# A two-block decoder kernel: the end of each RWKV head pair placed beside the beginning of the next, with one table for the weight products behind the steps

## The reference, cut to what matters

```python
w = -softplus(-(w0 + tanh(wd) @ w2)) - 0.5;  decay = exp(-exp(w))
a = sigmoid(a0 + ad @ a2)
kk = heads(k * k_k);  kk = kk * rsqrt(max(sum(kk * kk), 1e-24))
k = k * (1.0 + (a - 1.0) * k_a)
o = rwkv7_scan(r, decay, k, v, -kk, kk * a)     # state = state*w + sa*b + v*k, o = state @ r
mean = mean(o); var = mean(square(o - mean))    # per head of 64
o = (o - mean) * rsqrt(var + GN_EPS) * ln_w + ln_b
yb = (o + sum(r * k * r_k) * v) * silu(bz)
```

## Time and profile before

| | us |
|---|---|
| median of 3 runs | 3160.08 (3158.09 to 3163.82) |
| profiled execution | 3159.61 |
| its span, first to last instruction | 3157.7 |
| TensorE busy | 3028.3 (96%), mean granted clock 0.984 |
| DVE busy | 1664.5 (53%) |
| ACT busy | 1357.8 (43%) |

### The profile page before, as it was taken

The page is one execution under the profiler, slowest core; times in us unless marked ns, Lnnn a source line. Parts: engine busy times, 40 slices in busy tenths (PEclk is TensorE's granted clock), DMA queues, the critical chain, the costliest instruction groups (busy, mean ns, idle before and its releaser), DMA issues.

```text
span 3157.7 us, 44484 instructions
## 1 busy us (share of the span) xinstructions
PE 3028.3 (96%) x19042; PEld 2586.2 (82%) x19042; DVE 1664.5 (53%) x1975; ACT 1357.8 (43%) x1563; POOL 76.0 (2%) x186
## 2 busy tenths in 40 slices
PE   7999999889999999999999999999999999999998
PEld 6888877868998878879889879888888888888886
DVE  5555555547655555645455456655555444444444
ACT  5333333434454445444444444444444444444333
POOL 4000000000100000000000000000000000000000
PEclk9999999999999999999999999999999999999999
DMA  6333333336666555556655645666656666666554
GB/s 188 108 108 109 108 110 110 106 102 185 175 191 195 163 153 153 187 173 173 179 169 173 188 137 146 175 189 187 193 187 180 183 183 183 187 184 198 188 187 146
DMA packets 355098, 516.32 MB, mean 164 GB/s; under 512 B 18224, under 2 KB 137156, under 8 KB 354132
## 3 DMA queue, kind: packets, MB, share of 16 engines
q1 hardware_dynamic: 354132, 510.27, 53.8%
q0 software_dynamic: 768, 3.20, 0.4%
HBM read 511.29 MB, written 2.11 MB: 163 GB/s over the span
## 4 chain that ended last, share of the span: by engine, by line
PE 92%; ACT 4%; DVE 3%; issue 1%; DMA 0%; SPq 0%; DVEq 0%; ACTq 0%
PE gp L1361 20%; PE gp L1363 20%; PE gp L1362 20%; PE gp L1370 8%; PE gp L1371 8%; PE gp L1372 8%; PE ps L1522 4%; PE ps L1412 1%; PE ps L1483 1%; PE ps L1508 1%; ACT w_hi L548 1%; PE ps L1469 1%; DVE arena L877 1%; DVE w_lo L883 0%; ACT L540 0%
## 5 line engine op out<-in xcount | busy, mean ns | idle before, releaser
L883 DVE TENSOR_TENSOR w_lo<-w_raw,w_hi 128x1024 fp32r<-128x1024 f32 (+2 forms) x976 | 1168.2, 1202 | 944.5 <-ACT w_hi L548 943.1
L548 ACT ACTIVATE w_hi<-w_raw 128x1024 fp32r<-128x1024 f32 (+2 forms) x976 | 1012.6, 1040 | 1229.6 <-PE gp L1363 916.7
L1361 PE MATMUL gp<-w_hi,h_hi 128*128 128x512 f32 x1920 | 768.7, 400 | 0.0
L1362 PE MATMUL gp<-w_hi,h_lo 128*128 128x512 f32 x1920 | 758.3, 395 | 0.0
L1363 PE MATMUL gp<-w_lo,h_hi 128*128 128x512 f32 x1920 | 757.9, 395 | 0.0
L1370 PE MATMUL gp<-h_hi,w_hi 128*128 128x256 f32 x2080 | 613.9, 295 | 8.6 <-DVE w_lo L883 6.8
L1371 PE MATMUL gp<-h_lo,w_hi 128*128 128x256 f32 x2080 | 586.8, 282 | 0.0
L1372 PE MATMUL gp<-h_hi,w_lo 128*128 128x256 f32 x2080 | 586.2, 282 | 0.0
L1363 PEld LDWEIGHTS gp<-w_lo,h_hi 128*128 128x128 f32 x1920 | 360.2, 188 | 87.9
L1361 PEld LDWEIGHTS gp<-w_hi,h_hi 128*128 128x128 f32 x1920 | 360.3, 188 | 87.0
L1362 PEld LDWEIGHTS gp<-w_hi,h_lo 128*128 128x128 f32 x1920 | 360.4, 188 | 84.3
(11 more groups left out here) (282 smaller groups left out, 2024.7 us busy)
## 6 DMA issues: line engine op xcount, KB each, us to landing
w_raw<-in_w_in SPq DMA_DIRECT2D x384, 512.0 KB, 3.7
w_raw<-in_w_ffn_gate SPq DMA_DIRECT2D x88, 512.0 KB, 4.4
w_raw<-in_w_ffn_up SPq DMA_DIRECT2D x88, 512.0 KB, 4.3
w_raw<-in_w_ffn_down SPq DMA_DIRECT2D x88, 512.0 KB, 3.7
w_raw<-in_w_in SPq DMA_DIRECT2D x136, 256.0 KB, 3.2
w_raw<-in_w_in SPq DMA_DIRECT2D x128, 192.0 KB, 2.8
w_raw<-in_w_mem_kv SPq DMA_DIRECT2D x32, 512.0 KB, 4.0
w_raw<-in_w_o SPq DMA_DIRECT2D x32, 512.0 KB, 4.0
```

Source lines behind the costliest of these rows:

```text
L548: act.activation(w_hi[:, slot, 0:size], w_raw[:, slot, 0:size], ACT.Copy).then_inc(sem("hi_done"), 1)
L883: dve.tensor_tensor(w_lo[:, slot, 0:size], w_raw[:, slot, 0:size], w_hi[:, slot, 0:size].bitcast(F32), ALU.subtract)\
L1361: pe.matmul(o, xh, wh, start=(k == 0), stop=False)
L1362: pe.matmul(o, xl, wh, start=False, stop=False)
```

## The change

1. Each pair's part is cut in three functions on each engine: `pair_begin(p)` (lora, sigmoids, kk, root, decays, and on DVE the products up to `kr_ready`), `pair(p)` (products, levels, chunks), and the end. The end of pair p - 1 is spread: the mean, the deviation, its square, the variance and the second root stand inside `pair_begin(p)`; DVE's `pair_end(p - 1)` stands behind `k_read` of pair p, ACT's `y_hi` behind the g copy of level 1, DVE's `low_y` ahead of level 2. The bonus product goes ahead of the last output product, and DVE reads it at once.
2. The units of all pairs are one list of 128 units (512 quarters). `plan_fill` says how many quarters are dealt out by each step; TensorE takes them by quarters, ACT and DVE by the whole units that this number holds. Nothing drains between pairs.
3. `on_heads` makes each term for both heads before the next term.
4. The evacuation of a B block waits for `kr_ready` in place of `shift_read`, and buffers are placed anew in the arena.

The core of the diff:

```diff
+STEPS = ([("prod", 2)] + [(f"{s}{l}", q) for l in range(1, LEVELS) for s, q in (("g", 2), ("x", 3))]
+         + [(f"{s}{c}", q) for c in range(NC) for s, q in (("w", 1), ("u", 2), ("s", 2 if c < NC - 1 else 0))]
+         + [("o", 2), ("mean", 3), ("kk", 2), ("var", 10)])
+FIRST_STEPS = [("o", 5), ("kk", 6), ("var", 5)]
+def plan_fill():
+    upto, n = {}, 0
+    for p in range(-1, KB):
+        for step, quarters in FIRST_STEPS if p < 0 else STEPS:
+            n += quarters
+            upto[p, step] = n
+    return upto
...
+            def fill(p, step):
+                while todo and todo[0] - first_todo < upto[p, step] // 4:
+                    unit(todo.pop(0))
...
@@ scalar: evacuate
-                        act.wait_ge(sem("shift_read"), a)
+                        act.wait_ge(sem("kr_ready"), a)
@@ scalar
+            def pair_begin(p):
+                fill(p - 1, "o")
                 act.wait_ge(sem("lora_z"), p + 1)
                 act.activation(r_sg, psA[:, 0:T], ACT.Sigmoid, bias=g2("b_w0", p))
                 act.activation(r_aa, psA[:, T:2 * T], ACT.Sigmoid, bias=g2("b_a0", p)).then_inc(sem("sigmoids"), 1)
                 act.wait_ge(sem("kk_ready"), p + 1)
                 act.activation(r_sq, r_kk, ACT.Square).then_inc(sem("kk_sq"), 1)
-                fill()
+                if p:
+                    deviation(p - 1)
+                fill(p - 1, "kk")
                 act.wait_ge(sem("kk_sum"), p + 1)
                 root(r_rs, psB[:, 0:T], 0.0)
+                if p:
+                    variance(p - 1)
                 act.wait_ge(sem("mid_ready"), p + 1)
                 act.activation(r_e1[:, :, :], r_cm0[:, :, :], ACT.Exp, scale=-KAPPA)
                 act.activation(r_e2[:, :, :], r_cm0[:, :, :], ACT.Exp, scale=KAPPA).then_inc(sem("decays"), 1)
-                fill(4)
+                fill(p - 1, "var")
...
@@ vector: pair_begin
                 dve.tensor_scalar(r_kk, k, g2("b_k_k", p), None, ALU.mult).then_inc(sem("kk_ready"), 1)
+                if p:
+                    deviation(p - 1)
                 dve.wait_ge(sem("sigmoids"), p + 1)
...
-                fill()
...
+                fill(p - 1, "o")
                 inverse_root(r_rs, 1e-12)
...
-                fill(3)
+                dve.wait_ge(sem("kr_ready"), p + 1)
+                fill(p - 1, "var")
@@ vector: pair
                 dve.copy_predicated(r_akr[:, :, :], each(m_upper[:], NC, 2 * CHUNK), both(psC)).then_inc(sem("k_read"), 1)
+                if p:
+                    pair_end(p - 1)
                 for l in range(1, LEVELS):
-                    fill()
+                    if l == 2 and p:
+                        low_y(y_hi[:, p - 1, :], y_lo[:, p - 1, :], r_t)
...
+                    fill(p, f"x{l}")
@@ tensor
+            def on_heads(out, *terms):
+                for i, (left, right) in enumerate(terms):
                     for hh in heads:
-                        for i, (left, right) in enumerate(terms):
-                            ins = pe.matmul(...)
+                        ins = pe.matmul(...)
+            def pair_begin(p):
                 pe.matmul(psA[:, 0:T], w2a2[:, 0, cols], lora_x[:, :], start=True, stop=True)
                 pe.matmul(psA[:, T:2 * T], w2a2[:, 1, cols], lora_x[:, :], start=True, stop=True).then_inc(sem("lora_z"), 1)
-                fill(1)
+                fill(p - 1, "o")
+                if p:
+                    mean(p - 1)
+                    fill(p - 1, "mean")
                 pe.wait_ge(sem("kk_sq"), p + 1)
                 pe.matmul(psB[:, 0:T], blk[:], r_sq, start=True, stop=True).then_inc(sem("kk_sum"), 1)
-                fill(3.5)
+                fill(p - 1, "kk")
+                if p:
+                    variance(p - 1)
+                fill(p - 1, "var")
...
@@ tensor: the calls (ACT and DVE alike)
+            fill = planned_quarters()
+            pair_begin(0)
             for p in range(KB):
-                fill = fill_quarters([f"B{p + 1}", f"A{p}"] if p + 1 < KB else [f"A{p}", "gate_b0"])
-                pair(p, fill)
-                fill.drain()
+                pair(p)
+                if p + 1 < KB:
+                    pair_begin(p + 1)
+            fill(KB - 1, "o")
+            mean(KB - 1)
+            fill(KB - 1, "mean")
+            variance(KB - 1)
+            fill.drain()
```

More of the change, by code:

```diff
@@ L322, in filler, with planned, drain @@
             fill.drain = lambda: fill(len(todo))
+            return fill
+        upto = plan_fill()
+        def planned(unit):
+            todo = list(range(units_of("B1")[0], units_of("gate_b0")[-1] + 1))
+            def fill(p, step):
+                while todo and todo[0] - first_todo < upto[p, step] // 4:
+                    unit(todo.pop(0))
+            def drain():
+                while todo:
+                    unit(todo.pop(0))
+            first_todo = todo[0]
+            fill.drain = drain
             return fill
@@ L726, in pair, with deviation, variance, pair_end @@
                 act.activation(r_e2[:, :, :], r_cm0[:, :, :], ACT.Exp, scale=KAPPA).then_inc(sem("decays"), 1)
-                fill(4)
+                fill(p - 1, "var")
+            def deviation(p):
+                act.wait_ge(sem("dev_ready"), p + 1)
+                act.activation(r_dsq, r_dd, ACT.Square, scale=1.0 / 8).then_inc(sem("dev_sq"), 1)
+            def variance(p):
+                act.wait_ge(sem("var_done"), p + 1)
+                root(r_var, psC[:, T:2 * T], GN_EPS)
+            def pair_end(p):
+                act.wait_ge(sem("rwkv_t"), p + 1)
+                act.activation(y_hi[:, p, :], r_t, ACT.Copy).then_inc(sem("y_hi"), 1)
+            def pair(p):
+                fill(p, "prod")
                 for l in range(1, LEVELS):
@@ L730, in pair @@
                     act.activation(one_of_pair(r_g, l, 1), packed(psB, l), ACT.Copy).then_inc(sem("g_read"), 1)
-                    fill()
-                fill(4)
+                    if l == 1 and p:
+                        pair_end(p - 1)
+                    fill(p, f"g{l}")
+                for c in range(NC):
+                    fill(p, f"w{c}")
                 act.wait_ge(sem("o_done"), p + 1)
                 act.activation(r_o, psB[:, 0:T], ACT.Copy).then_inc(sem("o_read"), 1)
-                act.wait_ge(sem("dev_ready"), p + 1)
-                act.activation(r_sq, r_dd, ACT.Square, scale=1.0 / 8).then_inc(sem("dev_sq"), 1)
-                fill()
[L738 to L741, removed]
             act.wait_ge(sem("ident_ready"), 1)
@@ L1178, in _ @@
             fill.drain()
+            fill = planned(unit)
+            pair_begin(0)
             for p in range(KB):
-                fill = filler(unit, [f"B{p + 1}", f"A{p}"] if p + 1 < KB else [f"A{p}", "gate_b0"])
-                pair(p, fill)
-                fill.drain()
+                pair(p)
+                if p + 1 < KB:
+                    pair_begin(p + 1)
+            deviation(KB - 1)
+            pair_end(KB - 1)
+            low_y(y_hi[:, KB - 1, :], y_lo[:, KB - 1, :], r_t)
+            fill.drain()
             fill = filler(unit, ["gate_b"])
@@ L1374, in unit, with planned_quarters, fill, drain @@
                     ins.then_inc(sem("unit_used"), 1)
-            def fill_quarters(names):
-                todo = [(n, part) for name in names for n in units_of(name) for part in range(4)]
-                def fill(k=1):
-                    for _ in range(int(4 * k)):
-                        if todo:
-                            n, part = todo.pop(0)
-                            unit(n, part=part)
-                fill.drain = lambda: fill(len(todo))
+            def planned_quarters():
+                n0 = units_of("B1")[0]
+                todo = [(n, part) for n in range(n0, units_of("gate_b0")[-1] + 1) for part in range(4)]
+                total = len(todo)
+                def fill(p, step):
+                    while todo and total - len(todo) < upto[p, step]:
+                        n, part = todo.pop(0)
+                        unit(n, part=part)
+                def drain():
+                    while todo:
+                        n, part = todo.pop(0)
+                        unit(n, part=part)
+                fill.drain = drain
                 return fill
@@ L1510, in attention, with pair_begin @@
                     ins.then_inc(sem("pv_done"), 1)
-            def pair(p, fill):
-                heads = [slice(0, 64), slice(64, 128)]
-                chunk = lambda c: slice(c * CHUNK, (c + 1) * CHUNK)
-                def on_heads(out, *terms):
+            heads = [slice(0, 64), slice(64, 128)]
+            chunk = lambda c: slice(c * CHUNK, (c + 1) * CHUNK)
+            def on_heads(out, *terms):
+                for i, (left, right) in enumerate(terms):
                     for hh in heads:
-                        for i, (left, right) in enumerate(terms):
```

(7 more changed lines are left out.)

93 lines of the change are left out of this document (48 added, 45 removed).

## The result

| | before | after |
|---|---|---|
| median, us | 3159.26 (4 runs) | 3122.95 (4 runs, 3121.35 to 3126.69) |
| ratio | | 0.9887, 95% interval 0.9871 to 0.9902 |
| span of the profiled execution, us | 3157.7 | 3120.8 |
| granted clock | 0.984 | 0.990 |

The kernel is 36.3 us faster. The forecast was 3123. Lines have moved by the edit: L1370 is now L1444 (L1361 is L1435), L883 is L941, L548 is L585, L1522 is L1600, L1530 is L1612, L568 is L605.

A forecast was written before the change was run, and what follows sets the result against it. TensorE, busy 96% of the span, was taken as the bound, with idle time and slow clock to win. Gains of 24.1 + 6.7 + 4.9 - 0.4 + 3.0 - 1.6 = 36.7 us gave 3123 us, range 3094 to 3146.

The forecast's parts named there:

- The joint: Between head pairs: the kk_sum wait at L1530 goes, shorter w_lo waits replace it; seven joints fall from 57.5 to 33.4 us.
- what is late next: At the joints, TensorE waits for DVE's next w_lo, made only behind kr_ready: 1.9 to 4.7 us each, 23.2 in all.
- A: Rival, chance 0.11: the joint between pairs closes wholly because DVE's w_lo is in time; 3090 us.
- B: Rival, chance 0.17: the joint's wait changes name but keeps its size, w_lo late, 7 us a joint with clock; 3139 us.
- D: Rival, chance 0.05: nothing gained, kk_sq stays late at L1530 because a conversion stands ahead of the sigmoids; about 3160 us.
- C: Rival, chance 0.05: slower, DVE bounds the inside of the pair, TensorE waits for it at level 1 or 2; 3171 us.
- E: Rival, chance 0.02: each ACT table switch ahead of the first root costs about a second load, 18 us; 3141 us.
- Clock behind the joints: Half clock after the new joint waits: 1.7 us for five long ones, half for two short; 10.2 us, bounds 0 and 13.3.
- Part 2: ACT's evacuation of the B block moves to where TensorE has 5.4 us of steps until the next copy: 6.7 us gained.
- So the 6.7 us of rows 2 go: TensorE's seven waits at L1522 for ACT's copy L730, held up by the B block's evacuation, vanish: 6.7 us.
- Part 3: Alternating heads in on_heads shortens groups of small products with two or three terms: 0.6 us a pair, 4.9 over eight.
- Part 4: The ends: first pair loses 0.4 us, last gains 3.0 (waits 4.1, then about 2); inside even pairs 1.6 is lost.

The follow-up runs named there:

- experiment 1: The changed kernel with DVE's w_lo of step o moved right behind kk and one more unit's w_lo at the old place: 3094.5 us.
- experiment 2: The changed kernel with DVE's w_lo of step o left out there for pairs 1 to 7 and made in step var: 3149.3 us.
- experiment 8: The changed kernel with w_lo of steps o (earlier) and x5 (later) moved, one ACT conversion ahead of the root, conversions inside the last pair's end: 3083.9 us.
- experiment 6: The changed kernel with DVE's w_lo of step x5 moved behind its copy of u in chunk 0: 3122.6 us.
- experiment 5: The kernel before with only the new order of heads in on_heads: 3159.5 us against 3159.2, ratio 1.0002.
- experiment 4: The changed kernel with the old order in on_heads, all terms of one head and then of the other: 3125.4 us.

## Why the prediction was right, point by point

**The joint.** The step that carried it, "what is late next", holds: no wait at L1530's counterpart but the first pair's (2.7 us, forecast near 2.8), and seven waits for w_lo. Forecast 4.7, 2.4, 4.7, 1.9, 3.8, 1.9, 3.8; measured 3.98, 2.23, 4.87, 1.75, 3.18, 1.91, 3.06. Sum 21.0 for 23.2. Experiments 1 and 2 show the cause from both sides, and experiment 8 the part of it that the forecast gave to ACT's conversions. In the reasoning behind it the w_lo at step "o" was counted as part of DVE's chain; experiment 2 shows that at most joints DVE would have waited for ACT's root in its place.

**Rivals at the joint.** A (closes wholly) did not come true, but experiment 1 comes near it: 3094.5 us where A had 3090. B, D and C did not come: no wait at the levels, where DVE had its pair's end in time. Nor did E, the drain behind each table load that the Trainium skill (ScalarE: Activation LUTs, What ACT_TABLE_LOAD costs) states: the trace has the root at 207.77, 0.02 us behind the end of its table load (1.28 us from 206.47).

**Clock behind the joints.** Forecast 10.2 us, five losses of 1.7 and two halves. Measured five losses of about 1.7, 8.4 us, after pairs 0, 1, 2, 3 and 6; the wait of 3.18 us went free and that of 1.75 did not. The number was close, but which waits would pay was not foreseen, and their length does not say it: the sum was right in part by luck.

**Part 2, the evacuation.** The step "So the 6.7 us of rows 2 go" was wrong by half. They went at L730's counterpart, but 3.6 us came back as waits for the w copy (L1600 for DVE L1213), since I looked at what stands behind the evacuation on ACT and not at DVE, whose w_lo waits for the conversion behind it. Experiment 6 shows it for 3.0 of the 3.6 us.

**Part 3, the order.** The group times are right (0.16 us for 20 products, 0.16 for 12, 4.1 us in all for 4.9). That they would show in the time was wrong for the kernel before (experiment 5) and only partly so after (2.5 us by the medians, with 0 and 4.1 both within the noise, experiment 4).

**Part 4.** The last pair waits 4.1 and 2.1 us, as forecast; the first loses 0.2 more, for 0.4. The 1.6 us inside even pairs were over-sized: three waits of 0.1 us for a w copy; four of 0.3 us for w_lo ahead of the joints take up most of the rest.

**The sum.** By kind over the pairs: idle time of TensorE 63.1 to 34.9 us, 28.2 less (forecast 29.3); loss to half clock 17.8 to 12.8, 5.0 less (forecast 2.5); groups of small products 4.1 less (forecast 4.9). That is 37.3 us for a span shorter by 36.9, and the forecast's 36.7. So the total was met partly by errors of 1 to 2.5 us that cancel, and that the median fell within 0.1 us of the forecast is luck. A pair's period, forecast to fall from 78.4 to 73.5 us, fell to 72.2 (from 141.59 to 574.60 over six pairs): the table deals 62 quarters to a pair where the kernel before dealt 64, and the forecast left these 1.4 us out of the period. They are made elsewhere, so the total is not touched. Parts 1, 2 and the new placing of units were run together; apart from the order and TensorE's dealing none was timed alone.

## What to carry to other kernels

When a wait is taken away, count for each engine how far ahead its supply runs at that step and which instruction in its own order makes the next piece; here that arithmetic gave the new wait within 0.8 us at every joint, and making one w_lo of 1.2 us more at each joint, in an idle stretch of DVE, was worth 28 us more. A producer that waits for another engine held up the copy behind it (1.5 us, twice, in experiment 6), so put conversions for later use behind the copies that someone waits for now. Judge a small saving on TensorE only where TensorE does not wait: beside regular waits its clock can give the saving back (4.9 us for 4.5 in experiment 5).

## What the runs showed of the hardware that was not expected

- A saving of 4.5 us of TensorE's small products left the time where it was (ratio 1.0002, 0.9993 to 1.0011); in the traces half clock behind the nine waits took 4.9 us more, since the waits ended earlier and the clock did not come back earlier. Where the waits were nearly gone, the same order was worth about 4 us, to some 3 us.
- The same instructions with the same longer waits, behind the pairs, lost between 7.8 and 13.2 us to half clock from one traced kernel to another. So a difference of a few microseconds between two kernels can be clock alone.
- The wait's length does not decide alone whether half clock follows: 1.75 us was followed by it and 3.18 us was not, in one execution.
- What the order of the two heads' products is worth depends on the group: in groups of 8 (one product of two terms), two terms of one head and then two of the other took 0.385 us against 0.378 when alternated, so the order hardly mattered; in groups of 20 (two terms, then three) it was 0.89 against 0.73.
